# A decoder step on one core: the low weights of each down projection's third unit, split ahead of the low parts of the last five FFN tiles

## The reference

```python
D_MODEL, D_FF = 1024, 2816

def swiglu(h, w_gu, w_down):
    g, u = jnp.split(h @ w_gu, 2, axis=-1)
    return (jax.nn.silu(g) * u) @ w_down

x = x + 0.5 * swiglu(rmsnorm(x, p['ffn1_norm'][layer]), p['ffn1_w_gu'][layer], p['ffn1_w_down'][layer])
# mixer or attention
x = x + 0.5 * swiglu(rmsnorm(x, p['ffn2_norm'][layer]), p['ffn2_w_gu'][layer], p['ffn2_w_down'][layer])
```

## Time and profile before

| what | value |
|---|---|
| median of 3 runs | 2396.92 us |
| the three runs | 2396.23, 2396.92, 2401.48 us |
| profiled execution: its own time | 2401.84 us |
| its span | 2399.9 us |
| TensorE (PE) busy | 2309.9 us, 96% |
| VectorE (DVE) busy | 1660.2 us, 69% |
| ScalarE (ACT) busy | 1035.3 us, 43% |
| granted TensorE clock, mean | 0.978 |

### The profile page before, as it was taken

One profiled execution on the slowest core, in us unless ns is written; L12 is line 12 of the kernel. 1 busy time (PEld: TensorE's weight loads), 2 busy tenths in 40 slices (PEclk: granted clock), 3 DMA queues, 4 the chain that ended last, 5 costly groups with the idle time before them and its releaser, 6 DMA issues.

```text
span 2399.9 us, 45751 instructions
## 1 busy us (share of the span) xinstructions
PE 2309.9 (96%) x17219; PEld 2257.8 (94%) x17219; DVE 1660.2 (69%) x2599; ACT 1035.3 (43%) x1788; POOL 352.7 (15%) x312
## 2 busy tenths in 40 slices
PE   9999999989999999999999999999998899999997
PEld 8999999989999899999999999999997799999997
DVE  7999833668888753999952489996246459999622
ACT  5444522445665543444432344444236424444412
POOL 0000011214444422000002100000123140000011
PEclk9999999999999999999999999999999889999998
DMA  3222222335455422222222222222241012222122
GB/s 134 88 88 104 70 88 88 129 100 161 152 165 165 136 82 99 73 99 87 88 84 92 95 69 100 87 96 71 97 121 45 19 60 93 94 87 104 63 97 74
DMA packets 63651, 230.55 MB, mean 96 GB/s; under 512 B 7392, under 2 KB 7520, under 8 KB 63392
## 3 DMA queue, kind: packets, MB, share of 16 engines
q1 hardware_dynamic: 52560, 187.72, 23.1%
q0 software_dynamic: 10704, 41.10, 5.4%
q10 hardware_dynamic: 288, 0.37, 0.0%
HBM read 216.57 MB, written 14.56 MB: 96 GB/s over the span
## 4 chain that ended last, share of the span: by engine, by line
PE 72%; DVE 13%; issue 8%; ACT 5%; POOL 1%; DVEq 0%; DMA 0%; POOLq 0%; ACTq 0%
PE psum L492 34%; PE psum L566 23%; PE psum L529 8%; DVE hloB L1467 2%; DVE part L1472 1%; DVE wlo L1444 1%; DVE opraw_own L1434 1%; DVE opraw L1434 1%; DVE cacc L1649 1%; PE psum L746 1%; DVE wlo L1402 1%; ACT hhi L1001 1%; POOL probs L2118 1%; PE psum L913 1%; PE psum L725 1%
## 5 line engine op out<-in xcount | busy, mean ns | idle before, releaser
L1402 DVE TENSOR_TENSOR wlo<-wraw,whi 128x1024 fp32r<-128x1024 f32 x197 | 269.0, 1367 | 319.3 <-ACT whi L965 314.4
L965 ACT ACTIVATE whi<-wraw 128x1024 fp32r<-128x1024 f32 x189 | 200.0, 1058 | 628.3 <-PE psum L492 579.3
L566 PE MATMUL psum<-Blo,whi 128*128 128x288 f32 x1216 | 362.9, 298 | 0.0
L566 PE MATMUL psum<-Bhi,wlo 128*128 128x288 f32 x1216 | 360.6, 297 | 0.0
L566 PE MATMUL psum<-Bhi,whi 128*128 128x288 f32 x1216 | 358.8, 295 | 0.0
L492 PE MATMUL psum<-hhi,whi 128*128 128x288 f32 x1408 | 306.6, 299 | 13.8 <-DVE wlo L1402 12.7
L492 PE MATMUL psum<-hhi,wlo 128*128 128x288 f32 x1408 | 305.2, 298 | 0.0
L566 PE MATMUL psum<-Bhi,ophi_own 128*128 128x288 f32 x912 | 270.6, 297 | 11.6 <-DVE part L1472 7.6
L566 PE MATMUL psum<-Blo,ophi_own 128*128 128x288 f32 x912 | 269.0, 295 | 0.0
L566 PE MATMUL psum<-Bhi,oplo_own 128*128 128x288 f32 x912 | 268.2, 294 | 0.0
L492 PEld LDWEIGHTS psum<-hhi,whi 128*128 128x128 f32 x1408 | 228.3, 191 | 16.5 <-DVE wlo L1402 14.8
(11 more groups left out here) (308 smaller groups left out, 5107.9 us busy)
## 6 DMA issues: line engine op xcount, KB each, us to landing
wraw<-w SPq DMA_DIRECT2D x349, 512.0 KB, 3.4
A<-cum_rows POOLq DMA_DIRECT2D x16, 576.0 KB, 3.9
h0s<-ssm_state POOLq DMA_DIRECT2D x16, 512.0 KB, 4.9
h0T<-ssm_state_t POOLq DMA_DIRECT2D x16, 512.0 KB, 5.4
ssm_s<-h0s POOLq DMA_DIRECT2D x16, 512.0 KB, 3.8
x<-x_in SPq DMA_DIRECT2D x8, 288.0 KB, 6.8
y<-ybuf SPq DMA_DIRECT2D x8, 288.0 KB, 2.7
kv_kept<-cache_kv POOLq DMA_DIRECT2D x1, 1920.0 KB, 10.3
```

The lines of the kernel that those rows point to most:

```text
L566: last = pe.matmul(of_p[p], wt[:, cols], m[:, p, k, :], start=k == 0 and i == 0, stop=k == NK // 2 - 1 and i == 2)
L965: act.activation(whi[n % 2][:], wraw[RAW[n]][:], ACT.Copy).then_inc(weights_hi, 1)
L1402: dve.tensor_tensor(wlo[n % 2][:], wraw[RAW[n]][:], whi[n % 2][:].bitcast(F32), ALU.subtract).then_inc(weights_lo, 1)
```

## The change

VectorE's `split_lo` of the down projection's third unit is written between `hidden_lo(16)` and `hidden_lo(17)`, and no longer at the start of `residual`. This holds in all four FFNs (`per == 3` is true for the down projections alone).

```diff
@@ gate_up, seven(last=True), VectorE
                         for k in range(6, NF):
                             if k == 9:
                                 split_lo(n + 2 * NF + 1, 0)
+                            if k == 17:
+                                split_lo(n + 2 * NF + 2, 0)
                             hidden_lo(k)
@@ residual, VectorE
-                body(0, True, skip=2 if kwise else 0)
+                body(0, True, skip=2 if kwise else 1 if per == 3 else 0)
                 with dve.Fori(1, NK // 2 - 1) as i:
                     body(i)
```

## The result

The changed kernel takes 2377.62 us (median of 4 runs, 2375.45 to 2382.21), the kernel before 2397.93 us (4 runs, 2396.23 to 2401.48; the three listed ahead of the prediction and one of 2398.95). The ratio is 0.9916, with a 95% interval of 0.9897 to 0.9935. The forecast was 2377.3 us in a range of 2371.5 to 2384.5. The profiled execution took 2377.38 us, its span is 2375.3.

A forecast was written before the change was run, and what follows sets the result against it. TensorE, busy 2309.9 of 2399.9 us, was taken as the bound. Closing its stops (13.33 us) and regaining clock (6.75) sum to 20.08 us; 19.6 off the median 2396.92 gives 2377.3 us, range 2371.5 to 2384.5.

The forecast's parts named there:

- The cause of the stop: Third unit of each down projection: VectorE's late split, behind thirteen low parts, stops TensorE for 3.16 or 3.17 us.
- The hole's term: Between second and third unit of each down projection: TensorE's stop closes, 13.33 us over the four.
- The near tie: Third unit's start in down0: the split allows 287.99, TensorE is ready at 288.01, within 0.02 us.
- The 0.1 us behind the wait: Third unit's first pair: followed after 0.37 us, not 0.27; saved only if TensorE pulls the weight load ahead, sum then 20.5.
- The clock's term: Third units, slowed by a lower clock behind the stop: 2.53, 0, 1.53 and 2.69 us, together 6.75 us gained.
- Rival 1: The hole closes but the clock does not come back: only 13.3 us gained, 2383.6 us; chance 0.11.
- The pushed-back low parts and the fourth unit: Low parts 17 to 21 and fourth split stay in time, margins 0.3 and 0.4 us; cost 0, bound 1.14 per projection.
- rival 2: TensorE waits for low parts 17 to 21 or the fourth unit: 4.6 us go back, 2381.9 us; chance 0.07.
- The wait for the high weights: On VectorE ahead of the moved split: already over, weights ready at 285.61, 1.11 us before the split's place.
- Rival 3: ScalarE's high weights come late, holding VectorE's split and five low parts: slower, 2402.1 us if 1.3 us past break-even; chance 0.02.
- rival 4: Something downstream that does not move with TensorE swallows the gain: 2396.9 us; chance 0.03.
- The weight load: SyncE's load for the fifth unit: issued 3.35 us earlier, landed by 291.4, before TensorE frees the buffer at 292.9.

The follow-up runs named there:

- s19: Changed kernel with the third unit's split ahead of low part 19 instead of 17; 2383.10 us, ratio 0.9930 to the kernel before.
- fill: Kernel before, with 24 idle products on TensorE between second and third unit of each projection's first output tile; 2394.03 us, ratio 0.9972 to the kernel before.
- before_again: The kernel before, unedited, run once more with a profile; 2397.57 us in its one run.
- only3: Kernel before with the change in the last FFN alone, down0 to down2 as before; 2392.30 us, ratio 0.9975 to the kernel before.
- s16: Changed kernel with the third unit's split ahead of low part 16 instead of 17; 2378.72 us, ratio 0.9909 to the kernel before.
- s10: Changed kernel with the third unit's split ahead of low part 10 instead of 17; 2401.64 us, ratio 1.0015 to the kernel before.
- the second comparison: The changed kernel, unedited, run once more against the kernel before; 2375.43 us, ratio 0.9908, by the ratio 22 us less.

## Why the prediction was right, point by point

- **The cause of the stop.** VectorE's order, neither ScalarE nor a load. Right: the split's place alone moved the third unit's start, and in s19 it came 1.27 us behind the split's start, as in the kernel before.
- **The hole's term, 13.33 us.** Right: each third unit now starts 0.27 us behind the last pair, as forecast. The near tie held too: by the split's start (287.00 + 1.27) the third unit could begin at 288.27, and TensorE was free at 288.29. The 0.1 us behind the wait, which the prediction left inside the 5.09 us, was not saved: the unit's first weight load starts at 288.28, 0.01 us ahead of its pair, and the second pair still follows after 0.36 us.
- **The clock's term, 6.75 us.** Right in size for the profiled execution, and fill shows its cause. That the profiled execution came near the average is luck: in before_again the same four stops cost 8.00 us. In the eleven unchanged stops of three profiles (four in each of the kernel before, three in only3) the third unit lasted 5.09 once and 6.35 to 7.78 us ten times; the mean is 1.7 us over 5.09, so 6.9 us for four. Rival 1, that the clock would not come back, is ruled out by the clock of 1.00 behind all four seams.
- **The pushed-back low parts and the fourth unit.** Right: 0 was taken out of 0 to 1.14 us, and no row shows a wait there, so rival 2 falls. s16 showed how near the low parts are: one place earlier, low part 16 sets the third unit's start.
- **The wait for the high weights.** Not reached at 17 (ready at 285.89, wanted at 287.00). Rival 3 was a true mechanism at another place, as s10 shows.
- **Nothing downstream takes the gain (rival 4).** Right: from down3's eviction to the end it takes 141.89 us, and took 141.88 before.
- **The weight load** set off by the moved split was hidden: ScalarE started on the fifth unit at 293.38, when its buffer came free, and not later.
- **The total.** 20.08 us was right for the four places. I took 19.6 off the median, on the guess that the median execution had less of the clock's term than the profiled one. The measured 20.3 us, and 22 us in the second comparison, don't bear out that step; it was small, and the spread of single executions is wider than it. That the time itself was met within 0.3 us is partly luck: the fourth run moved the median of the kernel before up by 1.0 us, and the gain was 0.7 us larger than forecast.

## What to carry to other kernels

Where one engine prepares several operands for another in a fixed order, write down when each one is wanted, and put each preparation just ahead of that: here the split was wanted after low part 16, stood after low part 21, and five short instructions cost 3.3 us. Time is lost on either side of the best place: later, each place cost one low part (two places 1.33 us in s19), and a place well ahead of the input's arrival held everything queued behind it (a stop of 4.2 us in s10; the places between 10 and 16 were not run). A stop of TensorE is to be priced with the slower stretch behind it, here half as much again (6.75 on 13.33 us); read it from the length of the same work with and without it, and in more than one profile, since it differs from execution to execution.

## What the runs showed of the hardware that was not expected

- A stop of 3.16 or 3.17 us was followed by a stretch at half the clock in ten of eleven cases, long enough that 18 pairs of matmuls took 6.35 to 7.78 us and not 5.09. A stop of 3.29 us between down1 and down2 was followed by one in seven of nine, and the four stops of 4.2 us in s10 all were; the four stops of 1.16 to 1.17 us in s19 were followed by none. TensorE at work on useless products kept the full clock in four of four.
- The time from one fixed point to another differs between executions, mostly by what the clock took: by 8 us in the mixer (901.79 to 909.88 us) and by 1.5 us between down1 and down2 (413.7 or 415.2 us). From down3's eviction to the end all nine profiles show 141.9 or 142.0 us. The kernel's spread from run to run goes the same way: of its 39 executions beside the experiments the fastest (2391.59 us) has a mean granted clock of 0.982 and the slowest (2406.09 us) one of 0.975. Which stops in the mixer it comes from was not taken apart.
